# A fourth projection unit loaded ahead into its own place, and a new order on VectorE and ScalarE around decay and sparse scores

## The chip, the cores and the metric

The kernel runs on one core of a Trainium2 chip. The metric is the device time of one execution in microseconds (us), the median of three runs. The engines of the core work side by side, each with its own queue of instructions: TensorE (PE: matmuls; PEld: the loads of their stationary operand), VectorE (DVE), ScalarE (ACT), GpSimd (POOL) and SyncE (SP). SP and POOL issue the transfers (DMAs) from device memory that this case is about. Engines wait for each other through semaphores.

## What is computed

Two layers over 256 tokens of width 1024, all in fp32. The change lies in the first, whose shape is:

```python
mod = jax.nn.silu(c) @ mod_w + mod_b                  # shift, scale, gate, twice
h = rms_norm(x, g_pre_mix) * (1 + scale1) + shift1
(sc_b, sc_c, sc_x, q, k, v, z, xbc, dt_raw, gl_a, gl_b, gl_c) = split_columns(h @ w_in)
y_a = short_conv_mixer(sc_b, sc_c, sc_x, sc_conv_w) @ w_sc_out
y_b = stick_breaking_attention(q, k, v) @ w_sb_out     # log-sigmoid scores, cumulated, exp
y_c = mamba2_mixer(z, xbc, dt_raw, ...) @ w_ssm_out    # conv, silu, decay matrix, scores, y * silu(z), norm
merged = sigmoid(gl_a) * y_a + sigmoid(gl_b) * y_b + sigmoid(gl_c) * y_c
x = x + gate1 * rms_norm(merged @ w_o, g_post_mix)
h2 = rms_norm(x, g_pre_ffn) * (1 + scale2) + shift2
x = x + gate2 * rms_norm((silu(gt) * up) @ w_ffn_out, g_post_ffn)
```

The second layer has attention, pooling, and a mixture of single experts: for each token and each of 8 heads 16 rows of an expert table are fetched, multiplied with the token and added up.

## The kernel before

**Units of weights.** All weights of the projections come as units of 128 x 2048 fp32 values (1 MiB), in the order of the list ORDER: xbc 0 to 2, sc 0 to 2, qk 0 and 1, v, z 0 and 1, gl 0 to 11, then br 0 to 3 (output projections of the three branches), wo 0 to 3, and the feed-forward units gu and dn. Unit u lies in slot u % 3 of `ring`. SP loads a unit when the unit three before it is done (`load`, L422: it waits for `unit_done`, which TensorE raises once per unit). FRONT0 is the unit sc 0. The first three loads (`first_load`) wait for nothing.

**Three passes.** The xbc units are multiplied as plain fp32 (L619). From sc 0 to gl 11 each unit is split: ScalarE writes a rounded high half (`split_front`, L1216, in two halves), VectorE the remainder (`front_lo`, L1824, over the unit in the ring), and TensorE makes three products low x high, high x low, high x high (`proj_T`, lines L509 to L511, 48 matmuls of 256 columns each with their weight loads). ScalarE copies each result out of its accumulator bank (`copy_out`, L1199) and raises `evac`; TensorE may run two units ahead of that copy.

**Modulation.** `mod_w` is 48 further units of 1 MiB. VectorE multiplies each with silu(c) and sums (`mod_unit`: two `mod_dot`, L1747). Units 0 to 7 come among SP's first loads (`load_pair(0)` to `load_pair(3)`) and give the scale and shift of h: two columns of hT for each pair (`early_columns`), which ScalarE then makes from x (`hT_part`, L1187). From unit 8 on POOL loads them (`load_mods`, L1551) into the two buffers of `mod_ring`: unit m is issued when unit m-2 has been summed. Units 8 to 19 are needed by `modulation(8, 20)`, 20 to 27 later.

**The start.** `transposes(0)` brings x into eight chunks k; chunks 2j and 2j+1 of hT follow pair j. `xbc_part(j, *ks)` makes the matmuls of xbc j over the chunks ks. `products_in_pause(n, ...)` makes n plain fp32 products whose result nobody uses, so that TensorE has work where it would wait. Then ScalarE rounds all of hT (`hq_h`, L1250) and VectorE makes the rest (`hq_l`, L1828). After sc 0 come the 32 small matmuls for dt (L642).

**Order on VectorE and ScalarE.** It is written out by hand. VectorE goes through the convolution of xbc, dt, the short convolution, the sparse scores (`sbl`, `sba`), the decay (L1944 to L1958), y and its norm (`yc`, `ysq`), then the merging of the branches (L2030 to L2039) in the loop over br; between these stand the `front_lo` of the coming units and the `mod_unit`s. In the decay, VectorE makes 16 arguments from a matmul (`acs_mm`, L719/L720, signalled by `dec_arg`), ScalarE takes exp (L1315), TensorE makes the scores of B and C (`bc_mm`, after gl 7, when all 16 arguments are read), VectorE multiplies (L1958, `w_ready`), and TensorE makes y from it after gl 8 (L738, `y_mm`). The sum of squares (L748) follows gl 9. TensorE's br j needs the low half of its own unit (`split_br`) and from j = 2 on the merged result of br j-2; wo 0 needs merged 0 to 2 and its low half (`split_wo`, L2016).

ScalarE takes for the sparse scores Abs, Exp, then the split of gl 0, then Ln (`sb_log`), and only then copies z 0 out, with Silu.

Of the kernel before, what the change touches and what calls it, by code (L numbers as in the profile page):

```python
# [127 lines left out]
def build(nc, stream, mod_w, c_rows, small, x, band, final_g, experts, out):  # L128
    with ExitStack() as ctx:
# [144 lines left out]
        w_lo = [rounded(f"w_lo{s}", "areaB", s * UNIT, UNIT) for s in range(RING)]  # L274
        front_hi = [rounded(f"front_hi{n}", *at, UNIT)
                    for n, at in enumerate((("spare", 0), ("xn", 0), ("gate_area", 4096), ("areaB", 6144)))]
        ring_lo = [rounded(f"ring_lo{s}", "ring", s * UNIT, UNIT) for s in range(RING)]
        yc_h, yc_l = rounded("yc_h", "areaA", 2048, 4, T), rounded("yc_l", "areaA", 3072, 4, T)
# [120 lines left out]
        def _(sp):  # L399
# [12 lines left out]
            sp.dma_start(sm[:, 0:n_late], small[:, 0:n_late]).then_inc(small_in, 16)  # L412
            load_pair(1)
            first_load(0)
            load_pair(2)
            first_load(1)
            load_pair(3)
            first_load(2)
# [16 lines left out]
            for i in range(1, edge):  # L435
                for s in range(RING):
                    load(i, s, False)
# [36 lines left out]
        def _(pe):  # L474
            mm = nc.tensor.matmul

            def arrived(kind, j):
                u = AT[kind, j]
                if kind == "wq":
                    pe.wait_ge(*query_arrived(j))  # L480
                    return query_w[j]
                if (kind, j) == ("wo2", 2):
                    pe.wait_ge(wo2_in, 16)
                    return spare[:, :]
                pe.wait_ge(w_in[u % RING], 16 * (u // RING + 1))
                return slot[u % RING]
# [47 lines left out]
            def front_parts(u, half):  # L534

                if u == FRONT0:
                    pe.wait_ge(hq_lo_ready, 1)
                pe.wait_ge(front_lo_ready, 2 * (u - FRONT0) + half + 1)
                return front_high(u), ring_lo[u % RING]
# [85 lines left out]
            products_in_pause(5, 1, xn[:, 0, 0:T])  # L625
            xbc_part(0, 2, 3)
            xbc_part(1, 0, 1)
            products_in_pause(4, BX, xn[:, 0, 0:T])
            xbc_part(1, 2, 3)
            xbc_part(0, 4, 5)  # L630
            xbc_part(1, 4, 5)
            xbc_part(2, 0, 1)
            xbc_part(2, 2, 3)
            xbc_part(0, 6, 7)
            xbc_part(1, 6, 7)
            xbc_part(2, 4, 5, 6, 7)
# [497 lines left out]
        def _(act):  # L1134
# [66 lines left out]
            def split_hi(u, i=0):  # L1201

                act.wait_ge(w_in[u % RING], i * 16 + 16 * (u // RING + 1))
                if u >= SPLIT0 + RING:
                    act.wait_ge(unit_done, i * RING + (u - RING + 1))
                A(w_hi[u % RING], slot[u % RING], ACT.Identity).then_inc(hi_ready, 1)  # L1206

            def split_front(u):

                act.wait_ge(w_in[u % RING], 16 * (u // RING + 1))  # L1210
                if u > FRONT0:
                    act.wait_ge(unit_done, u - RING + 1)
                if u == AT["gl", 9]:
                    act.wait_ge(acs_mm, 2)
                for half in halves_of_unit:
                    A(front_high(u)[:, half], slot[u % RING][:, half], ACT.Identity).then_inc(front_hi_ready, 1)  # L1216

            def split_br(j):

                u = AT["br", j]  # L1220
                act.wait_ge(w_in[u % RING], 16 * (u // RING + 1))
                A(br_hi[j], slot[u % RING][:, UNIT // 2:], ACT.Identity).then_inc(front_hi_ready, 1)

            def split_wo(j):

                u = AT["wo", j]
                act.wait_ge(w_in[u % RING], 16 * (u // RING + 1))
                for half in (slice(0, UNIT // 2), slice(UNIT // 2, UNIT)):
                    A(wo_hi[j][:, half], slot[u % RING][:, half], ACT.Identity).then_inc(front_hi_ready, 1)
# [21 lines left out]
            n = 0  # L1251
            for j in range(3):
                if j == 2:
                    split_front(FRONT0)
# [27 lines left out]
            step.wait()  # L1282
            A(sbl, sbl, ACT.Ln, bias=1.0).then_inc(sb_log, 1)
            for j in range(2):
                copy_out("z", j, zg[:, 2 * j:2 * j + 2, :], func=ACT.Silu, bank=n % 2)
                if j == 0:
                    split_front(n + 3)
                n += 1
            for b in range(6):
# [259 lines left out]
        def _(pool):  # L1549
# [8 lines left out]

            load_mods(MOD_SP, MOD_FRONT + 2)
# [92 lines left out]
        def _(dve):  # L1652
# [166 lines left out]
            def front_lo(kind, j):  # L1819

                u = AT[kind, j]
                for h, half in enumerate(halves_of_unit):
                    dve.wait_ge(front_hi_ready, 2 * (u - FRONT0) + h + 1)
                    V.tensor_tensor(ring_lo[u % RING][:, half], slot[u % RING][:, half],  # L1824
# [4 lines left out]

            for k in range(4):  # L1830
# [5 lines left out]
                for b in range(6):  # L1836
                    w = c_("ssm_w", 4 * b + k, 4 * b + k + 1)
                    if (k, b) == (0, 4):
                        front_lo("sc", 0)
# [121 lines left out]
            mod_unit(21)  # L1961
            front_lo("gl", 10)
            mod_unit(22)
# [10 lines left out]
            mod_unit(23)  # L1974
# [30 lines left out]
            mod_units(24, 26)  # L2005
# [568 lines left out]
```

## Time and profile before

| | us |
|---|---|
| median of 3 runs | 1218.07 |
| the runs | 1217.13, 1218.07, 1776.78 |
| the profiled execution, its own time | 1217.03 |
| its span, first to last instruction | 1215.4 |
| granted clock of TensorE, mean of full speed | 0.972 |
| TensorE busy (matmul) | 1072.5 |
| VectorE busy | 875.8 |
| ScalarE busy | 517.5 |

One of the three runs was disturbed. The page gives busy times and the chain that ended last; the trace behind it can be asked for windows, waits and single instructions. In what follows a time like 160.2 us counts from the start of the span of the profiled execution. The durations of matmuls are modelled: their starts are the sounder figure.

### The profile page before, as it was taken

The numbers are of one execution on the slowest core, as the hardware profiler recorded it, in microseconds if no ns is written. First come the engines' busy times: TensorE is split into PE (matmuls) and PEld (weight loads), VectorE is DVE, ScalarE is ACT, GpSimd is POOL, SyncE is SP. The second block draws the span as 40 slices with busy tenths as digits, with TensorE's granted clock in tenths as the row PEclk, the third lists the DMA queues.
The fourth block names the chain that finished last, engine by engine and source line by source line (L and its number), as shares of the span: only waits on it lengthen the run. The fifth ranks groups of instructions, "written<-read, shape, count | busy, mean of one in ns | idle before, by whom it ended". The sixth has DMA issues, their size and how long they took to land.

```text
span 1215.4 us, 14124 instructions
## 1 busy us (share of the span) xinstructions
PE 1072.5 (88%) x4834; PEld 715.7 (59%) x4834; DVE 875.8 (72%) x1802; ACT 517.5 (43%) x1156; POOL 339.2 (28%) x326
## 2 busy tenths in 40 slices
PE   3899979999999999998999999977968878769776
PEld 3899969878999989765565555422323323223222
DVE  5668789977888887737797758668577586685455
ACT  3338443364333345435544344433434334334344
POOL 0000100031000002203544545634434535334320
PEclk9899999999999999999999999999999998999998
DMA  9756966565888882557999999999999999999994
GB/s 380 301 194 228 366 252 242 210 250 204 313 308 321 316 318 108 212 208 289 421 410 421 423 419 421 421 421 422 421 421 422 421 421 423 420 422 421 420 422 197
DMA packets 57946, 414.10 MB, mean 341 GB/s; under 512 B 6432, under 2 KB 6432, under 8 KB 8352
## 3 DMA queue, kind: packets, MB, share of 16 engines
q0 software_dynamic: 43632, 313.02, 63.0%
q1 hardware_dynamic: 14112, 100.10, 21.9%
q8 instruction: 30, 0.49, 0.2%
q10 hardware_dynamic: 144, 0.26, 0.1%
q14 instruction: 28, 0.23, 0.1%
HBM read 412.30 MB, written 1.05 MB: 340 GB/s over the span
## 4 chain that ended last, share of the span: by engine, by line
PE 53%; DMA 31%; DVE 9%; ACT 5%; issue 1%; POOL 0%; SPq 0%; ACTq 0%; DVEq 0%; POOLq 0%
PE ps L1064 15%; PE ps L509 8%; PE ps L510 8%; PE ps L511 8%; DMA areas_seam<-in_experts,idx 6%; DMA gate_area<-in_experts,idx 6%; DMA spare<-in_experts,idx 6%; PE ps L495 4%; DMA ring<-in_stream 3%; DMA mod_ring<-in_experts,idx 3%; DMA ring<-in_experts,idx 3%; DMA ring<-in_experts,part_buf 2%; PE ps L765 1%; PE ps L991 1%; PE ps L619 1%
## 5 line engine op out<-in xcount | busy, mean ns | idle before, releaser
L1485 ACT ACTIVATE act<-now 128x1 f32<-128x1 f32 x256 | 50.7, 198 | 264.3 <-DVE now L2369 262.0
L1064 PE MATMUL ps<-areaB,c_row 128*128 128x512 f32 x232 | 116.1, 633 | 26.1 <-ACT c_row L1493 26.1
L1493 ACT ACTIVATE c_row<-small,act 128x128 f32<-128x128 f32 x256 | 102.8, 402 | 16.3 <-ACT act L1489 0.8
L1747 DVE CUSTOM_DVE_ANT_0 mod_ring<-mod_ring,c_row 128x1024 f32<-128x1024 f32 x84 | 99.1, 1219 | 14.6 <-DMA mod_ring<-in_mod_w 14.5
L1064 PE MATMUL ps<-ring,c_row 128*128 128x512 f32 x192 | 92.8, 614 | 14.4 <-ACT c_row L1493 13.8
L1623 POOL DMA_INDIRECT areaB<-in_experts,idx x58 | 65.3, 1126 | 124.5 <-PE ps L1064 65.8
L509 PE MATMUL ps<-hT_h,w_lo 128*128 128x256 f32 x352 | 99.1, 282 | 0.8 <-DVE hid_l L2062 0.8
L511 PE MATMUL ps<-hT_h,w_hi 128*128 128x256 f32 x352 | 98.9, 281 | 0.0
L510 PE MATMUL ps<-hT_l,w_hi 128*128 128x256 f32 x352 | 98.8, 281 | 0.0
L2369 DVE CUSTOM_DVE_ANT_0 areaB<-areaB,xn 128x1024 f32<-128x1024 f32 x58 | 70.7, 1224 | 37.3 <-DMA areaB<-in_experts,idx 37.2
L1064 PEld LDWEIGHTS ps<-areaB,c_row 128*128 128x128 f32 x232 | 43.6, 197 | 90.9 <-ACT c_row L1493 47.1
L1206 ACT ACTIVATE w_hi<-ring 128x2048 fp32r<-128x2048 f32 x41 | 78.4, 1913 | 40.7 <-PE ps L511 38.0
L509 PE MATMUL ps<-hq_h,ring_lo 128*128 128x256 f32 x304 | 88.9, 293 | 4.6 <-DVE ring_lo L1824 3.5
L1064 PE MATMUL ps<-gate_area,c_row 128*128 128x512 f32 x156 | 75.4, 606 | 13.9 <-ACT c_row L1493 13.9
L510 PE MATMUL ps<-hq_l,front_hi 128*128 128x256 f32 x304 | 87.3, 287 | 0.0
L511 PE MATMUL ps<-hq_h,front_hi 128*128 128x256 f32 x304 | 87.0, 286 | 0.0
L2369 DVE CUSTOM_DVE_ANT_0 ring<-ring,xn 128x1024 f32<-128x1024 f32 x48 | 58.4, 1225 | 31.2 <-DMA ring<-in_experts,idx 31.1
L1760 DVE TENSOR_TENSOR w_lo<-ring,w_hi 128x2048 fp32r<-128x2048 f32 x30 | 68.7, 2292 | 16.3 <-ACT w_hi L1206 16.3
L1489 ACT ACTIVATE act<-act,gate_buf 128x1 f32<-128x1 f32 x256 | 75.4, 295 | 9.3
L1555 POOL DMA_DIRECT2D mod_ring<-in_mod_w x22 | 11.8, 538 | 235.1 <-DVE modT L1747 235.1
L1064 PEld LDWEIGHTS ps<-ring,c_row 128*128 128x128 f32 x192 | 35.5, 194 | 66.2 <-issue 35.8
L1623 POOL DMA_INDIRECT ring<-in_experts,idx x47 | 54.9, 1168 | 65.9 <-PE ps L1064 52.2
(436 smaller groups left out, 2591.7 us busy)
## 6 DMA issues: line engine op xcount, KB each, us to landing
ring<-in_stream SPq DMA_DIRECT2D x75, 1024.0 KB, 5.0
mod_ring<-in_mod_w POOLq DMA_DIRECT2D x40, 1024.0 KB, 5.3
gate_area<-in_mod_w SPq DMA_DIRECT2D x3, 1024.0 KB, 14.7
areaB<-in_mod_w SPq DMA_DIRECT2D x3, 1024.0 KB, 24.6
gate_area<-in_stream SPq DMA_DIRECT2D x3, 1024.0 KB, 13.0
mod_ring<-in_mod_w SPq DMA_DIRECT2D x2, 1024.0 KB, 7.6
small<-in_small SPq DMA_DIRECT2D x1, 1352.0 KB, 28.6
c_row<-in_c_rows SPq DMA_DIRECT2D x2, 512.0 KB, 17.4
```

The source lines that it names most:

```text
L509: mm(o, lhs[1], rhs[0], start=start, stop=False, **kw)
L510: mm(o, lhs[0], rhs[1], start=False, stop=False, **kw)
L511: return mm(o, lhs[0], rhs[0], start=False, stop=stop, **kw)
L1064: last = mm(ps[:, B3 + 2 * b + t, :], spread_w[n // FEW % 2][:, n % FEW, :], row[ROW_OF[n]][:, D + 512 * b:D + 512 * b + 512], start=first ...
L1206: A(w_hi[u % RING], slot[u % RING], ACT.Identity).then_inc(hi_ready, 1)
L1485: A(weight, now[n // FEW % 4][:, here], ACT.Gelu).then_inc(gelu_done, 1)
L1489: step(A(weight, weight, ACT.Identity, scale=gate_h[h % 2][:, t, n % TOPK:n % TOPK + 1]))
L1493: A(spread_w[n // FEW % 2][:, n % FEW, :], c_("ident"), ACT.Identity, scale=weight)\
L1623: pool.indirect_dma_start(row[ROW_OF[n]], None, experts, bass.IndirectOffsetOnAxis(ap=idx[:, n:n + 1], axis=0))\
L1747: V.tensor_tensor_reduce(w, w, silu, 1.0, 0.0, ALU.mult, ALU.add, column).then_inc(mod_summed, 1)
L1760: V.tensor_tensor(w_lo[s], slot[s], w_hi[s].bitcast(F32), ALU.subtract).then_inc(lo_dve, 1)
L2369: V.tensor_tensor_reduce(u, u, xn[:, t, :], 1.0, 0.0, ALU.mult, ALU.add, now[n // FEW % 4][:, n % FEW:n % FEW + 1]).then_inc(dot_done, 1)
```

## The change

- sc 0 gets a place of its own, `fourth` in areaB at 6144 (the place of `a_rep`, which is written only later), and its load stands among the first loads, behind the last pair of modulation units; it signals `wo2_in`. `w_arrived(u)` gives the semaphore and count for each unit. The next load of slot 0 is that of qk 0, still issued when sc 0 is done.
- SP's first loads: xbc 0 now before pair 1, xbc 1 and 2 before pair 2.
- TensorE's xbc parts are ordered by chunks: all three units get chunks 0 to 3, then 4 and 5, then 6 and 7; the pause products are 3, 3 and 3 instead of 5 and 4.
- ScalarE splits sc 0 before it copies xbc out; z 0 is copied (without Silu) before the Ln of the sparse scores, z 1 after the split of gl 1, and one Silu goes over both.
- POOL waits for `unit_done` 3 (all xbc units) before it loads modulation unit 8.
- VectorE makes the low half of gl 8 before the decay arguments. Units 19 and 20 no longer stand between arguments and products. The new places: 19 after the low half of gl 9, 20 to 22 between `split_br(0)` and `split_br(1)`, 23, 24, 25 in the branch loop. 26 and 27 stay.

```diff
+        fourth = cut(areaB, 6144, UNIT)
+        fourth_lo = rounded("fourth_lo", "areaB", 6144, UNIT)
...
+        def w_arrived(u):
+
+            if u == FRONT0:
+                return wo2_in, 16
+            return w_in[u % RING], 16 * (u // RING + 1) - (16 if u > FRONT0 and u % RING == FRONT0 % RING else 0)
...
             sp.dma_start(sm[:, 0:n_late], small[:, 0:n_late]).then_inc(small_in, 16)
+            first_load(0)
             load_pair(1)
-            first_load(0)
+            first_load(1)
+            first_load(2)
             load_pair(2)
-            first_load(1)
             load_pair(3)
-            first_load(2)
+            sp.dma_start(fourth, stream[FRONT0]).then_inc(wo2_in, 16)
...
-            for i in range(1, edge):
-                for s in range(RING):
-                    load(i, s, False)
+            for n in range(FRONT0 + 1, RING * edge):
+                load(n // RING, n % RING, False)
...
             xbc_part(0, 0, 1)
-            products_in_pause(5, 1, xn[:, 0, 0:T])
             xbc_part(0, 2, 3)
+            products_in_pause(3, 1, xn[:, 0, 0:T])
             xbc_part(1, 0, 1)
-            products_in_pause(4, BX, xn[:, 0, 0:T])
             xbc_part(1, 2, 3)
-            xbc_part(0, 4, 5)
-            xbc_part(1, 4, 5)
+            products_in_pause(3, BX, xn[:, 0, 0:T])
             xbc_part(2, 0, 1)
             xbc_part(2, 2, 3)
-            xbc_part(0, 6, 7)
-            xbc_part(1, 6, 7)
-            xbc_part(2, 4, 5, 6, 7)
+            products_in_pause(3, 2, xn[:, 0, 0:T])
+            for j in range(3):
+                xbc_part(j, 4, 5)
+            for j in range(3):
+                xbc_part(j, 6, 7)
...
+            split_front(FRONT0)
             for j in range(3):
-                if j == 2:
-                    split_front(FRONT0)
                 copy_out("xbc", j, xbc_raw[:, 2 * j:2 * j + 2, 3:], bank=(0, 1, BX)[j])
...
             split_front(AT["gl", 0])
-            step.wait()
-            A(sbl, sbl, ACT.Ln, bias=1.0).then_inc(sb_log, 1)
             for j in range(2):
-                copy_out("z", j, zg[:, 2 * j:2 * j + 2, :], func=ACT.Silu, bank=n % 2)
+                if j == 1:
+                    split_front(n + 2)
+                copy_out("z", j, zg[:, 2 * j:2 * j + 2, :], bank=n % 2)
                 if j == 0:
-                    split_front(n + 3)
+                    act.wait_ge(act_step, step.n)
+                    A(sbl, sbl, ACT.Ln, bias=1.0).then_inc(sb_log, 1)
                 n += 1
+            act.wait_ge(evac, n)
+            step(A(zg, zg, ACT.Silu))
...
+            pool.wait_ge(unit_done, 3)
             load_mods(MOD_SP, MOD_FRONT + 2)
...
+            front_lo("sc", 0)
             for k in range(4):
...
+            front_lo("gl", 7)
             mod_unit(18)
-            front_lo("gl", 7)
+            front_lo("gl", 8)
...
-            front_lo("gl", 8)
-            mod_units(19, 21)
             dve.wait_ge(bc_mm, 1)
             for h in range(8):
-                if h == 4:
-                    front_lo("gl", 9)
...
-            mod_unit(21)
+            front_lo("gl", 9)
+            mod_unit(19)
             front_lo("gl", 10)
-            mod_unit(22)
             dve.wait_ge(y_mm, 1)
...
             front_lo("gl", 11)
-            mod_unit(23)
...
             split_br(0)
-            mod_units(24, 26)
+            mod_units(20, 23)
             split_br(1)
...
             for j in range(4):
                 if j in (1, 2):
                     split_br(j + 1)
+                if j == 1:
+                    mod_unit(23)
+                if j == 2:
+                    mod_unit(24)
                 if j == 3:
+                    mod_unit(25)
                     split_wo(0)
```

## Rows read from the trace of the kernel before

**Rows 1.** Page: the chain that ended last, by engine, share of the span.

```profile
PE 53%; DMA 31%; DVE 9%; ACT 5%; issue 1%; POOL 0%; SPq 0%; ACTq 0%; DVEq 0%; POOLq 0%
```

**Rows 2.** Windows: length, busy us (xcount) by engine, granted clock, DMA share, GB/s.

```profile
760.00:1215.00 455.00, 356.89 (x730) 135.97 (x728) 298.18 (x709) 179.74 (x562) 183.87 (x171) 0.95 0.98 407
```

**Rows 3.** Two waits of TensorE, 100 to 180 us: total us, times, longest.

```profile
PE ps L509 <- ACT areaA L1199: 1.0, 1, 1.0
...
PE ps L738 <- DVE areaB L1958: 7.2, 1, 7.2
```

**Rows 4.** Windows of the front stages, same columns.

```profile
160.00:201.60 41.60, 33.98 (x270) 31.91 (x269) 40.60 (x73) 17.15 (x17) 2.64 (x5) 0.92 0.62 224
201.60:246.20 44.60, 43.97 (x246) 37.79 (x245) 43.48 (x63) 14.77 (x16) 1.58 (x3) 1.00 0.61 227
60.00:160.00 100.00, 98.85 (x801) 96.20 (x799) 72.05 (x109) 55.54 (x66) 5.82 (x11) 0.98 0.71 270
```

**Rows 5.** Timeline of the start: start us, us, engine, line, operation [idle before].

```profile
23.95 1.02 ACT L1187 ACTIVATE hT<-ps,cols 128x256 f32<-128x256 f32 x2 [2.65 <-DVE cols L1786]
...
26.50 1.23 DVE L1747 CUSTOM_DVE_ANT_0 areaB<-areaB,c_row 128x1024 f32<-128x1024 f32 x1
...
31.47 1.23 DVE L1747 CUSTOM_DVE_ANT_0 areaB<-areaB,c_row 128x1024 f32<-128x1024 f32 x1 [2.05 <-DMA areaB<-in_mod_w]
...
32.56 15.70 PE L619 MATMUL ps<-hT,ring 128*128 128x256 f32 x72
...
36.97 1.02 ACT L1187 ACTIVATE hT<-ps,cols 128x256 f32<-128x256 f32 x2 [6.44 <-DVE cols L1786]
...
39.97 2.29 DVE L1828 TENSOR_TENSOR hq_l<-hT,hq_h 128x2048 fp32r<-128x2048 f32 x1 [3.09 <-ACT hq_h L1250]
...
51.79 0.55 PE L509 MATMUL ps<-hq_h,ring_lo 128*128 128x256 f32 x1 [3.52 <-DVE ring_lo L1824]
```

**Rows 6.** Windows around two waits, then two matmuls of the chain.

```profile
54.00:57.00 3.00, 3.00 (x16) 3.00 (x15) 3.00 (x7) 1.15 (x2) 0.00 (x0) 0.50 0.06 25
...
179.80:182.00 2.20, 2.13 (x12) 1.55 (x14) 2.20 (x4) 0.01 (x1) 0.00 (x0) 0.50 0.60 242
...
52.34 0.21 PE ps L510
...
57.57 0.12 PE ps L511
```

**Rows 7.** ScalarE's copy of z 0, from its timeline.

```profile
107.53 0.60 ACT L1199 ACTIVATE areaA<-ps 128x512 f32<-128x512 f32 x1
```

**Rows 8.** A wait of VectorE, 60 to 246 us: total us, times, longest.

```profile
DVE mod_ring L1747 <- DMA mod_ring<-in_mod_w: 7.5, 4, 3.0
```

**Rows 9.** The mod_ring loads: landing times, one issue on POOL, its first product.

```profile
DMA to landing us min/median/max: 5.0/6.5/9.1
...
120.41 0.53 POOL L1555 DMA_DIRECT2D mod_ring<-in_mod_w  x1 [11.99 <-DVE modT L1747]
...
127.26 1.23 DVE L1747 CUSTOM_DVE_ANT_0 mod_ring<-mod_ring,c_row 128x1024 f32<-128x1024 f32 x1 [3.01 <-DMA mod_ring<-in_mod_w]
```

**Rows 10.** VectorE's timeline, then two pieces of the chain.

```profile
139.07 2.35 DVE L1824 TENSOR_TENSOR ring_lo<-ring,front_hi 128x1024 fp32r<-128x1024 f32 x2
...
160.20 0.48 DVE L1944 SCALAR_TENSOR_TENSOR areaB<-ps,dtb,small 128x256 f32<-128x256 f32 x1 [3.48 <-PE ps L720]
...
227.92 2.35 DVE L2016 TENSOR_TENSOR ring_lo<-ring,wo_hi 128x1024 fp32r<-128x1024 f32 x2
...
167.76 1.13 DVE mod_ring L1747
...
172.34 2.60 DVE areaB L1958 x8
```

**Rows 11.** Chain of work before gl 5, and behind wo 1.

```profile
140.76 0.44 PE ps L691 x4
...
241.90 4.88 DMA ring<-in_stream
```

More of the change, by code:

```diff
@@ L277, in build, with front_slot, front_low @@
         ring_lo = [rounded(f"ring_lo{s}", "ring", s * UNIT, UNIT) for s in range(RING)]
+        fourth_lo = rounded("fourth_lo", "areaB", 6144, UNIT)
+        def front_slot(u):
+            return fourth if u == FRONT0 else slot[u % RING]
+        def front_low(u):
+            return fourth_lo if u == FRONT0 else ring_lo[u % RING]
+        def w_arrived(u):
+            if u == FRONT0:
+                return wo2_in, 16
+            return w_in[u % RING], 16 * (u // RING + 1) - (16 if u > FRONT0 and u % RING == FRONT0 % RING else 0)
         yc_h, yc_l = rounded("yc_h", "areaA", 2048, 4, T), rounded("yc_l", "areaA", 3072, 4, T)
@@ L482, in arrived @@
                 if (kind, j) == ("wo2", 2):
-                    pe.wait_ge(wo2_in, 16)
+                    pe.wait_ge(wo2_in, 32)
                     return spare[:, :]
-                pe.wait_ge(w_in[u % RING], 16 * (u // RING + 1))
+                pe.wait_ge(*w_arrived(u))
                 return slot[u % RING]
@@ L538, in front_parts @@
                 pe.wait_ge(front_lo_ready, 2 * (u - FRONT0) + half + 1)
-                return front_high(u), ring_lo[u % RING]
+                return front_high(u), front_low(u)
             def proj_T(kind, j):
@@ L1201, in split_hi @@
             def split_hi(u, i=0):
-                act.wait_ge(w_in[u % RING], i * 16 + 16 * (u // RING + 1))
+                act.wait_ge(w_in[u % RING], i * 16 + w_arrived(u)[1])
                 if u >= SPLIT0 + RING:
@@ L1208, in split_front @@
             def split_front(u):
-                act.wait_ge(w_in[u % RING], 16 * (u // RING + 1))
+                act.wait_ge(*w_arrived(u))
                 if u > FRONT0:
@@ L1215, in split_front @@
                 for half in halves_of_unit:
-                    A(front_high(u)[:, half], slot[u % RING][:, half], ACT.Identity).then_inc(front_hi_ready, 1)
+                    A(front_high(u)[:, half], front_slot(u)[:, half], ACT.Identity).then_inc(front_hi_ready, 1)
             def split_br(j):
                 u = AT["br", j]
-                act.wait_ge(w_in[u % RING], 16 * (u // RING + 1))
+                act.wait_ge(*w_arrived(u))
                 A(br_hi[j], slot[u % RING][:, UNIT // 2:], ACT.Identity).then_inc(front_hi_ready, 1)
@@ L1226, in split_wo @@
                 u = AT["wo", j]
-                act.wait_ge(w_in[u % RING], 16 * (u // RING + 1))
+                act.wait_ge(*w_arrived(u))
                 for half in (slice(0, UNIT // 2), slice(UNIT // 2, UNIT)):
@@ L1823, in front_lo @@
                     dve.wait_ge(front_hi_ready, 2 * (u - FRONT0) + h + 1)
-                    V.tensor_tensor(ring_lo[u % RING][:, half], slot[u % RING][:, half],
+                    V.tensor_tensor(front_low(u)[:, half], front_slot(u)[:, half],
                                     front_high(u)[:, half].bitcast(F32), ALU.subtract).then_inc(front_lo_ready, 1)
@@ L1837, in _ @@
                     w = c_("ssm_w", 4 * b + k, 4 * b + k + 1)
-                    if (k, b) == (0, 4):
-                        front_lo("sc", 0)
                     if k == 0:
```

## The prediction

> **What bounds the kernel now.** I began with the page: the chain that ended last [rows 1]. TensorE carries just over half of the chain, the DMAs under a third, VectorE 9%. An average like that hides stages, so I cut the span next. In the window of the gather stage, from 760 us to the end, the DMA share is 0.98 at 407 GB/s [rows 2]: there the transfers of expert rows set the time, their bytes are fixed, and only when they start can move. Everything the change touches lies before 250 us, so its worth is how much earlier (or later) that part ends; the feed-forward stage and the gathers then pass the shift on unchanged. That is my assumption for all that follows.
>
> In the first 250 us, who waits for whom is short to tell. TensorE waits three times: 3.5 us for the low half of sc 0, 1.0 us for ScalarE's copy of z 0, 7.2 us for VectorE's decay products [rows 3, 5]. Windows by stage show the other side of it: from 60 to 160 us TensorE is busy 98.9 of 100 us and VectorE only 72, but from 160.0 to 201.6 VectorE is busy 40.6 of 41.6 and from 201.6 to 246.2 it is busy 43.5 of 44.6, while TensorE is busy 44.0 of that [rows 4]. So the first stage is TensorE's, and the stage from the decay to the output projection is VectorE's, with TensorE only just kept fed. Time that TensorE wins before 160 us can be kept; time that it wins after 160 us is kept only if VectorE ends earlier too.
>
> **Part 1: sc 0 in a place of its own.** Before, its load can be issued only when xbc 0 has freed the slot; ScalarE and VectorE split it only after that, and TensorE, done with xbc at 48.26, starts on it at 51.79, 3.52 us late [rows 5]. What would the new order of loads do? The 1 MiB loads go through in the order of issue at about 420 GB/s, 2.5 us each: modulation units 5 and 6 stand two loads apart in the queue and their first products start at 26.50 and 31.47, 5.0 us apart [rows 5]. The three xbc units and two pairs now stand ahead of the last pair, so the last modulation unit lands one load (2.5 us) later than before, and the last columns of hT come 2.5 us later: before they start at 36.97, after at about 39.5, ready by 40.6. Does TensorE wait for them? Its xbc work is the same 96 passes plus the same 9 pause products (5+4 before, 3+3+3 after) of 2 passes each at 0.217 us (15.70 us for 72 [rows 5]). The second pair of columns started at 23.95 before [rows 5]; its unit too lands one load later, but VectorE had come late to it, so the first of them is there at about 25.1. From then 106 passes remain, 23.0 us: the end is 48.1, the same as before, and the passes that need the last columns begin at 42.9, 2.3 us after these are there. hT's copy (1.9 us, to 42.5), its low half (2.3 us, to 44.9) and the first low half of sc 0 (to 46.1) also fit under it. So sc 0 starts at 48.1: 3.7 us gained.
>
> The pause costs more than itself. After it the granted clock stood at 0.50, the 1.2 GHz level, until about 57.2 us; matmuls of sc 0 follow each other at 0.21 us and then at 0.12 [rows 6]. Some 25 of its 48 ran at the slow pace: 25 x 0.09 = 2.3 us; with the long first one 2.5. Without the pause I take the clock to stay up. Part 1 is worth 3.7 + 2.5 = 6.2 us at 60 us. Behind it sc 1 and sc 2 (issued as before, at about 46 and 48) share the DMAs with the modulation units 8 and 9, which now wait for unit_done 3 on POOL's queue: 4.2 MB at 420 GB/s from 48 us are in by 58, and sc 2 is wanted at 63. Nothing is late.
>
> **Part 2: z and sparse scores on ScalarE.** The copy of z 0 now precedes the logarithm and its table load; before it ended at 108.1 behind them [rows 7] and TensorE waited 1.0 us [rows 3]. After: no wait. But the logarithm ends some 0.5 us later, the separate Silu over zg is one ACTIVATE of about 1.1 us more, and on VectorE modulation units 11 and 12 then end 1.0 us later, so the loads of 13 and 15 (each issued when its buffer is free) land 1 us later. VectorE was already waiting on such loads four times, 7.5 us [rows 8]. The low half of gl 5 stands behind unit 15 and was started 1.7 us ahead of TensorE (139.07 [rows 10], against the transposes ahead of gl 5 at 140.76 [rows 11]); with the sum and the load each 1 us later it is now about 0.9 late. I take the 1.0 us as given back: 0, with a bound of -1.0.
>
> **Part 3: the decay on VectorE.** The low half of gl 8 (2 halves, 2.3 us) moves from behind the decay arguments into the 3.5 us that VectorE waits for TensorE before 160.2 [rows 10]: cover enough. Units 19 and 20 (4 dots, 4.6 us [rows 10]) and the low half of gl 9 leave the way to the decay products, so these are there 5.2 us (2 x 2.60 [rows 10]) after the scores of B and C, before gl 8 ends on TensorE. The 7.2 us wait goes; so does the slow clock behind it (0.50 at 180 us [rows 6]), 1.5 us (16 + 16 passes of small products at twice their time, 4.6 us in place of about 3.1); and 0.4 us ahead of the sums of squares. By TensorE alone this is worth 9 us.
>
> VectorE's account says otherwise. From the first decay argument (160.20) to the first low half of wo 0 (229.1 [rows 10]) it has 68.9 us. The change takes 2.3 us out (gl 8), and adds nothing: units 19 to 25 stood in this stretch before and stand in it after, only later (20, 21, 22 between the two first branch splits, 23, 24, 25 in the branch loop). It adds two waits. First 1.3 us for the matmuls of B and C, because VectorE now comes there with nothing between. Then the three units in a row: mod_ring has two buffers, the load of unit 22 is issued only when unit 20 is summed, some 0.8 us after it, and lands 6.4 us later (the row: issued at 120.41, first product at 127.26, 6.85 us; median of all 6.5 [rows 9]). Unit 21 covers 2.3 us of it, so VectorE stands 0.8 + 6.4 - 2.3 = 4.9 us. Bounds: 0.8 + 5.0 - 2.3 = 3.5, and 0.8 + 9.1 - 2.3 = 7.6 from the shortest and longest landing. Sum: 68.9 - 2.3 + 1.3 + 4.9 = 72.8 us, 3.9 more than before; with the 0.35 us that TensorE was behind VectorE here, 3.5. The Trainium skill gives a fit for such a load in "DMA: Bandwidth & Descriptors", Anatomy of one DMA: about 2.0 us plus bytes over 436e3. It comes to 4.4 us for 1 MiB, no load of this row group was that fast, and by it the sum would be 2.0 us smaller.
>
> TensorE meanwhile finishes gl 11 some 8 us earlier, and stands in the branch stage: 2.4 us for the low half of br 1, 2.5 and 1.7 us for the merges, and about 5 us for the first half of wo 0. Only the last reaches the end. The pauses of 3.5 and of 7.2 us both had the clock at 0.50 behind them [rows 6], so I expect wo 0 to begin at 1.2 GHz. Price: between 1.5 us (the decay pause) and 2.5 (the first pause), I take 2.1. Behind it the chain is as before: wo 1 frees the slot, gu 0 loads in 4.9 us [rows 11].
>
> **Sum.** -6.2 (part 1) + 0 (part 2) + 3.5 (VectorE) + 2.1 (clock) = -0.6 us. Against the profiled run of 1217.03 us (span 1215.4) that is 1216.4; the two undisturbed timed runs lie 0.1 and 1.0 above the profiled one, so I forecast 1217.0 for the median. The likeliest case's own range is 1214 to 1219.
>
> **The rivals.**
> - *The early start is kept.* Unit 22 lands in time for unit 21's end, or the clock stays up in wo 0, or both: -0.6 - 4.9 - 2.1 = -7.6, so 1209.4 to 1215. For it: the DMA share was only 0.6 in these windows [rows 4]. Against: VectorE did wait for such loads with one unit in hand.
> - *TensorE is the bound and all its waits count.* 6.2 + 1.0 + 7.2 + 1.5 + 0.4 = 16.3: 1200.7. Against it: VectorE has 2 us of idle time in the 86 us of [rows 4].
> - *Slower: unit 22 comes late.* If it lands 9.1 us after issue as the longest [rows 9], VectorE stands 7.6 us and the sum is -0.6 + 2.7 = +2.1, with the clock's price at its upper bound 0.4 more: 1217.0 + 2.7 + 0.4 = 1220.1. It decides from a landing of 7.0 us on; POOL's loads then share with br 2 and br 3 of SP's queue, which speaks for it.
> - *Part 1 does nothing.* The last columns of hT are more than 2.3 us later than reckoned, or sc 1 then stalls instead: -0.6 + 6.2, 1222.6.
>
> **How the numbers follow.** Likeliest 0.50; early start kept 0.23; TensorE the bound 0.08; unit 22 late 0.13; part 1 without effect 0.06. The range 1209 to 1221 leaves out the second rival and the last, 0.14, and the tails. Two per cent, about what a measurement of this kernel can tell from no change, is 24 us, more than any case moves: faster 0.03, same 0.95, slower 0.02 stand for what I have not thought of.
>
> **What would show it.** Part 1: TensorE without a wait at 48 us, clock 1.00 from 46 to 54, sc 0's copy out near 54. Part 3: no wait before the decay products; in its place a wait of VectorE for a mod_ring load of 4 to 5 us shortly after the first branch split, and TensorE waits before br 2, br 3 and wo 0, the last with the clock at 0.5 behind it. The forecast is wrong if VectorE's stretch from the first decay argument to the first low half of wo 0 is under 70 us, or if sc 0 does not start by 49 us.

## The result and the profile after

| us | before | after |
|---|---|---|
| median | 1216.47 (20 runs, 1213.09 to 1776.78) | 1218.99 (20 runs, 1215.32 to 1222.07) |
| the profiled execution, its own time | 1217.03 | 1217.65 |
| its span | 1215.4 | 1215.8 |
| granted clock, mean | 0.972 | 0.973 |

One run of before (1776.78) and one of a_spread below (2730.70) were disturbed, and the ratios leave them out. The ratio after to before is 1.0021, 95% interval 1.0012 to 1.0029: the change costs 2.5 us. The forecast was 1217.0 within 1209 to 1221, a change of -0.6 us; the range holds, the sign doesn't. The gain of the first part is there, and the two losses that the forecast set against it are there too. When the load of gu 0 is issued, after is still ahead of before. What the forecast lacked is that this load, taken as unchanged, now takes 3.6 us longer.

The two profiled executions lie closer together (0.6 us) than the medians. They serve to see where time goes; what the change costs is read from the ratio.

The page's chain that ended last, by engine, has moved from TensorE to VectorE (compare [rows 1]: PE 53, DVE 9):

```profile
PE 50%; DMA 31%; DVE 12%; ACT 4%; issue 2%; POOL 0%; SPq 0%; ACTq 0%; POOLq 0%; DVEq 0%
```

Windows of after: length, busy us (xcount) of PE, PEld, DVE, ACT, POOL, granted clock, DMA share, GB/s. They answer to [rows 4] and to the first of [rows 6].

```profile
60.00:160.00 100.00, 99.70 (x812) 96.78 (x811) 78.09 (x123) 62.30 (x72) 5.83 (x11) 0.99 0.71 266
160.00:201.60 41.60, 38.41 (x296) 36.23 (x295) 35.75 (x59) 15.49 (x17) 2.12 (x4) 1.00 0.60 225
201.60:246.20 44.60, 34.48 (x171) 28.40 (x170) 40.81 (x59) 10.18 (x11) 2.65 (x5) 0.96 0.65 238
46.00:54.00 8.00, 8.00 (x62) 7.74 (x60) 6.23 (x14) 3.21 (x4) 1.26 (x2) 1.00 0.79 308
54.00:57.00 3.00, 3.00 (x29) 3.00 (x28) 2.28 (x3) 2.13 (x3) 0.00 (x0) 1.00 1.03 437
```

From 46 to 57 us TensorE has no gap, and its granted clock is 1.00 where it was 0.50. In the third row TensorE has 34.5 us of work in 44.6, 9.5 us less than before in that window: it stands there now. The waits of TensorE, 40 to 262 us, say for whom (total us, times, longest):

```profile
PE ps L525 <- DVE ring_lo L2030: 5.0, 1, 5.0
PE ps L781 <- DVE hT_l L2058: 4.1, 2, 2.6
PE ps L810 <- DVE xn L1725: 3.9, 2, 3.3
PE ps L764 <- DVE areaB L1987: 1.8, 1, 1.8
PE ps L525 <- DVE ring_lo L2015: 1.4, 1, 1.4
```

The 7.2 and 3.5 us of [rows 3, 5] are gone. In their place stand 5.0 us for the low half of wo 0, 4.1 for the merges, 1.8 ahead of the sums of squares (0.4 before), 1.4 for br 1, and 3.3 us of the third row behind wo, where it was 0.17 before. The last is TensorE waiting for what follows gu 0's high half. Single instructions of after, VectorE first, then GpSimd, then ScalarE (start us, us, engine, line, operation [idle before]):

```profile
153.15 0.49 DVE L1963 SCALAR_TENSOR_TENSOR areaB<-ps,dtb,small 128x256 f32<-128x256 f32 x1 [3.48 <-PE ps L736]
...
196.97 1.23 DVE L1766 CUSTOM_DVE_ANT_0 mod_ring<-mod_ring,c_row 128x1024 f32<-128x1024 f32 x1 [4.34 <-DMA mod_ring<-in_mod_w]
...
224.41 2.35 DVE L2030 TENSOR_TENSOR ring_lo<-ring,wo_hi 128x1024 fp32r<-128x1024 f32 x2
...
238.92 0.53 POOL L1573 DMA_DIRECT2D mod_ring<-in_mod_w  x1 [13.16 <-DVE modT L1766]
...
247.87 1.92 ACT L1222 ACTIVATE w_hi<-ring 128x2048 fp32r<-128x2048 f32 x1 [5.76 <-DMA ring<-in_stream]
```

And four pieces of the chain that ended last (start us, us, what): the start of wo 0, one of its later matmuls, and the load of gu 0.

```profile
225.78 0.77 PE ps L525
226.55 0.43 PE ps L526
...
229.17 0.23 PE ps L527
...
239.33 8.46 DMA ring<-in_stream
```

At the issue of gu 0's load after is 2.6 us ahead of before (239.33 against 241.90 [rows 11]). The load then takes 8.46 us in place of 4.88, and when ScalarE makes the high half of gu 0 (247.87; before 246.86) the kernel is 1.0 us behind. The same instructions before:

```profile
242.42 0.53 POOL L1555 DMA_DIRECT2D mod_ring<-in_mod_w  x1 [31.43 <-DVE modT L1747]
...
246.86 1.92 ACT L1206 ACTIVATE w_hi<-ring 128x2048 fp32r<-128x2048 f32 x1 [2.64 <-DMA ring<-in_stream]
```

Before, GpSimd's load of modulation unit 28 was issued at 242.42, 0.5 us behind that of gu 0. After, it is issued at 238.92, 0.4 us ahead of it. Measured from the low half of wo 0, GpSimd's issue hasn't moved (14.5 us behind it in both, since VectorE sums unit 26 in the same place); SyncE's has, from 13.98 to 14.92 us, since TensorE goes through wo 0 and wo 1 more slowly (below).

### The profile page after: what moved, and what is told of

Same layout as the page of the kernel before. It is cut to its first block, busy times and chain, and to the rows that moved or that the text cites. A ratio compares the mean times of both kernels' runs of the same rounds, so it can differ in the third digit from the quotient of the medians.

```text
span 1215.8 us, 14136 instructions
## 1 busy us (share of the span) xinstructions
PE 1072.7 (88%) x4834; PEld 714.9 (59%) x4834; DVE 876.1 (72%) x1802; ACT 518.7 (43%) x1157; POOL 340.4 (28%) x326
## 3 DMA queue, kind: packets, MB, share of 16 engines
HBM read 412.30 MB, written 1.05 MB: 340 GB/s over the span
## 4 chain that ended last, share of the span: by engine, by line
PE 50%; DMA 31%; DVE 12%; ACT 4%; issue 2%; POOL 0%; SPq 0%; ACTq 0%; POOLq 0%; DVEq 0%
PE ps L1080 15%; PE ps L525 8%; PE ps L526 7%; PE ps L527 7%; DMA areas_seam<-in_experts,idx 6%; DMA gate_area<-in_experts,idx 6%; DMA spare<-in_experts,idx 6%; PE ps L511 4%; DMA mod_ring<-in_experts,idx 3%; DMA ring<-in_experts,idx 3%; DMA ring<-in_experts,part_buf 2%; DMA ring<-in_stream 2%; PE ps L635 2%; DMA gate_area<-in_mod_w 1%; DVE mod_ring L1766 1%
## 5 line engine op out<-in xcount | busy, mean ns | idle before, releaser
L1080 PE MATMUL ps<-ring,c_row 128*128 128x512 f32 x192 | 95.7, 630 | 14.3 <-ACT c_row L1511 13.7
L525 PE MATMUL ps<-hq_h,ring_lo 128*128 128x256 f32 x288 | 83.1, 289 | 0.1
```

The lines of the kernel that those rows point to most:

```text
L525: mm(o, lhs[1], rhs[0], start=start, stop=False, **kw)
L1080: last = mm(ps[:, B3 + 2 * b + t, :], spread_w[n // FEW % 2][:, n % FEW, :], row[ROW_OF[n]][:, D + 512 * b:D + 512 * b + 512], start=first ...
```

## The experiments

Three theories stood behind the runs. **A**, the forecast's account: part 1 pays, and VectorE's late load of unit 22 and the slow clock of wo 0 take it back. **B**: the loads of unit 28 and of gu 0 collide, 3 to 4 us that A doesn't have. **C**, for later runs: the stage from the decay to wo 0 is bound by VectorE's work, or by its idle time, or by TensorE. Every ratio is against runs of before on the same chip; the instants are those of one profiled execution each. The difference of two ratios has an interval of its own. From the intervals of the table I estimate 1.7 to 2.0 us either way for the kernels made from after against after, and 2.7 to 3.1 us for those made from p1 among each other.

| kernel | median us | ratio to before, 95% | first decay argument | low half of wo 0 | high half of gu 0 |
|---|---|---|---|---|---|
| before | 1216.5 | 1 | 160.20 | 227.92 | 246.86 |
| after | 1218.99 | 1.0021 (1.0012, 1.0029) | 153.15 | 224.41 | 247.87 |
| p1 | 1211.35 | 0.9952 (0.9932, 0.9971) | 154.14 | 221.89 | 240.78 |
| p12 | 1211.75 | 0.9954 (0.9938, 0.9971) | 154.00 | 221.73 | 240.55 |
| p3 | 1227.14 | 1.0076 (1.0057, 1.0094) | 160.74 | 234.80 | 258.54 |
| a_spread | 1214.37 | 0.9978 (0.9967, 0.9990) | 154.04 | 220.88 | 244.26 |
| a_hold | 1221.86 | 1.0040 (1.0027, 1.0052) | 154.30 | 225.87 | 246.09 |
| a_issue | 1216.92 | 1.0003 (0.9990, 1.0016) | 152.79 | 224.76 | 244.42 |
| a_both | 1210.96 | 0.9958 (0.9944, 0.9972) | 153.46 | 220.27 | 240.37 |
| p1_g8 | 1207.79 | 0.9924 (0.9907, 0.9941) | 154.12 | 219.59 | 238.39 |
| g8_coll | 1210.92 | 0.9951 (0.9937, 0.9966) | 154.62 | 220.08 | 241.25 |
| g8_m19 | 1208.87 | 0.9936 (0.9920, 0.9951) | 159.04 | 222.19 | 240.91 |
| v_less | 1209.35 | 0.9948 (0.9933, 0.9963) | 153.44 | 220.81 | 239.74 |

### Part 1 alone, part 3 alone, parts 1 and 2

**p1**: the kernel before with the place of sc 0, the order of loads and of xbc, and GpSimd's wait; VectorE's order of decay and units, and ScalarE's of z, as before.

> Part 1 alone on the kernel before: sc 0 in its own place, the new order of the first loads and of the xbc parts, POOL's wait; VectorE's and ScalarE's later order as before. Theory A (VectorE's order after 160 us, with its wait for unit 22, gives the gain of part 1 back): this kernel keeps the 6 us, about 1210.5 against 1216.5, and wo 1 ends near 235.7 instead of 241.9. Theory C (the early start itself is worth nothing at the end, or later stages absorb it): no difference from before within 1 us.

5.8 us faster than before (0.9952), with all of the three instants of the table some 6.0 us earlier: 6.06, 6.03, 6.08. What part 1 gains before 60 us is carried through whole.

**p3**: only VectorE's new order on the kernel before.

> VectorE's order alone on the kernel before (gl 8 ahead of the decay arguments, units 19 to 25 later). Theory A: no wait for the decay products, but the stretch from the first decay argument to the first low half of wo 0 grows from 68.9 to about 72.8 us and wo 0 starts with the clock at half: 4 to 6 us slower than before. Theory B (the loss is made at the end of wo, where gu 0's load now shares the DMAs with unit 28's): 3 to 4 us more on top, gu 0 landing 8 us after its issue, so 8 to 9 us slower. Theory C (the order is worth its 7 us of TensorE): faster by up to 7 us.

1.0076, 9.2 us slower. VectorE waits 5.6 us for unit 22, and the low half of wo 0 is 6.9 us later than before; from there to gu 0's high half it is 23.7 us in place of 18.9, 4.8 us more. So VectorE's new order loses in two places, before wo 0 and behind it: A and B together, and part 3 is what makes the whole change slow. Part 1 and part 3 add up to -5.8 + 9.2 = +3.4, near the +2.5 of the whole.

**p12**: p1 with ScalarE's order of z and the sparse scores.

```diff
-            step.wait()
-            A(sbl, sbl, ACT.Ln, bias=1.0).then_inc(sb_log, 1)
             for j in range(2):
+                if j == 1:
+                    split_front(n + 2)
-                copy_out("z", j, zg[:, 2 * j:2 * j + 2, :], func=ACT.Silu, bank=n % 2)
+                copy_out("z", j, zg[:, 2 * j:2 * j + 2, :], bank=n % 2)
                 if j == 0:
+                    act.wait_ge(act_step, step.n)
+                    A(sbl, sbl, ACT.Ln, bias=1.0).then_inc(sb_log, 1)
-                    split_front(n + 3)
                 n += 1
+            act.wait_ge(evac, n)
+            step(A(zg, zg, ACT.Silu))
```

> The first part and the second together (the copy of z 0 ahead of the logarithm, one Silu over zg), VectorE's order as before; the first part alone ran at 1211.35 us. Theory A (the prediction's step: the 1.0 us is given back on the way to gl 5): 1211.4, and the first decay argument starts at 154.0 to 154.3 as with the first part alone (154.14). Theory B (it is kept, since the changed kernel's first decay argument stood 7.05 us earlier than before, where the first part gives 6.1): 153.2 to 153.4, and 1210.5 us. Told apart too by TensorE's wait for ScalarE near 113 us: none under B.

0.9954 against 0.9952: part 2 is worth nothing that these runs can tell, as forecast. The reason is another than the forecast's. The wait of 1.0 us for z 0's copy, which part 2 was to win, isn't there in p1 any more. In its place TensorE waits 0.8 us at 113 us for ScalarE's copy of gl 0, and in p12 it is 0.7 us (in after, with the same order on ScalarE, there is none). At gl 5, where the forecast had the gain given back, p12 shows no wait. The 7.05 us at the first decay argument of after was one execution: in the kernels with part 1 but without part 2 this instant lies between 153.44 and 154.62 (g8_m19 apart, for a reason told below), in those with both between 152.79 and 154.30.

### Is the wait for unit 22 what VectorE's order costs?

**a_spread**: after, with unit 20 put ahead of the sums of squares, and 21 and 22 left between the branch splits.

```diff
             front_lo("gl", 11)
+            mod_unit(20)
             dve.wait_ge(ysum_mm, 1)
...
-            mod_units(20, 23)
+            mod_units(21, 23)
```

> The changed kernel with unit 20 moved ahead of the wait for the sum of squares, so that only 21 and 22 stand between the first two branch splits and unit 22's load is issued earlier. Theory A: VectorE's 4.3 us wait for unit 22 goes, wo 0 starts 4 us earlier, the wait ahead of it is under 1.5 us and the clock stays up: 5 to 7 us faster than the changed kernel, about 1212.5. Theory B (only the collision of gu 0 and unit 28 counts): wo 1 ends earlier, but unit 28 is issued earlier by as much, the 8.5 us landing stays: at most 4 us faster.

0.9978, 5.2 us faster than after by the ratios. VectorE has no wait for unit 22 any more, and from the first decay argument to the low half of wo 0 it needs 66.8 us, after 71.3: the 4.3 us of that wait are the 4.4 us saved. TensorE's wait before wo 0 stays 5.0 us, against what I expected. It has nothing to do with unit 22. In after the merge of br 1 ends at 214.2, when TensorE starts br 3; VectorE then has a split of br 3 (1.14), unit 24 (2.3), merge 2 (4.6), unit 25 (2.3) and half a split (1.15), 11.4 us, and TensorE some 6.5 us for br 3. So I put this wait down to the units placed in the branch loop: the two units are 4.6 of VectorE's 11.4 us. That is read from the trace; no run moved these units alone.

### The collision of two loads

**a_hold**: after, with GpSimd issuing the loads of units 28 and 29 together, only behind its own part of gu 0.

```diff
-            load_mods(MOD_SP, MOD_FRONT + 2)
+            load_mods(MOD_SP, MOD_FRONT)
...
             split_lo(SPLIT0)
+            load_mods(MOD_FRONT, MOD_FRONT + 2)
```

> The changed kernel with the loads of units 28 and 29 held on POOL until ScalarE has made gu 0's high half, so that gu 0 has the DMAs to itself. Theory A: wo 1's end is what counts, the load is 5 us as before or little more: under 1 us of difference from the changed kernel. Theory B: gu 0 lands in 5 us instead of 8.5, everything behind it comes 3.5 us earlier: about 1215.5 against 1219.

1.0040, slower than after by 2.3 us. gu 0 itself is cured: its load takes 4.8 us, and the high half comes 20.2 us behind the low half of wo 0 (after 23.5). But the two held loads are then issued at 250.9 and meet the load of gu 1, issued at 251.83 and landed 9.3 us later. The high half of gu 1 waits until 261.17 (with after's distance of 12.9 us to that of gu 0 it would be 259.0), and TensorE waits 2.4 us at 263.7. The collision was moved by one unit, not removed; this run didn't separate the theories.

**a_issue**: the same idea, cleaner.

```diff
-            load_mods(MOD_SP, MOD_FRONT + 2)
+            load_mods(MOD_SP, MOD_FRONT)
+            pool.wait_ge(*w_arrived(SPLIT0))
+            load_mods(MOD_FRONT, MOD_FRONT + 2)
```

> The changed kernel, and GpSimd issues the load of modulation unit 28 only when gu 0 is in; units 28 and 29 then follow one by one as their buffers come free. Theory B (the collision of unit 28's load with gu 0's costs 3 us): gu 0 lands 4.9 us after its issue, its high half starts near 244.8 instead of 247.9, 1215.9 us. Theory A (what was lost there is not the order of the two loads but the total traffic): gu 0 still takes over 7 us, 1219.

1.0003: 2.2 us better than after by the ratios. The load of gu 0 takes 4.66 us (expected 4.9), the two held loads are issued together at 245.01 and not one by one, and from the low half of wo 0 to gu 0's high half it is 19.7 us in place of 23.5. B is confirmed in place by the trace, and 2.2 us agrees with its 3 us within the interval:

```profile
239.68 4.66 DMA ring<-in_stream
```

**a_both**: a_spread and a_issue together.

> The changed kernel with unit 20 ahead of the sums of squares, units 21 and 22 around the second branch split, and unit 28's load only when gu 0 is in. If the two losses are separate they add up: 4.6 (first, alone 1214.4) and 2.2 to 3.1 (second, alone 1216.9), 1211.3 to 1212.2 us, and what is left above the first part with gl 8 moved (1207.8) is the wait of 5.0 us before wo 0 with its slow clock. If they are one and the same loss: 1214.4.

0.9958: 7.7 us better than after, where the two alone gave 5.2 and 2.2. The losses are separate and add up within the intervals, and this kernel, with after's order of the decay and the branch loop, is as fast as p1. To p1_g8 below, 2.0 us remain at gu 0's high half, and another 1.5 us come behind it, in a stretch told at the end.

**g8_coll** turns it around: in a kernel without the collision (p1_g8, below) SyncE waits until unit 28's load has been issued. So that it can, GpSimd raises `pool_go` behind each load in place of ahead of it; nothing else waits for `pool_go`.

```diff
+                if n == SPLIT0:
+                    sp.wait_ge(pool_go, MOD_FRONT + 1 - MOD_SP)
...
-                        pool.sem_inc(pool_go, 1)
                         pool.dma_start(cut(mod_ring, n * UNIT, UNIT),
                                        mod_w[bass.ds(2 * i + n, 1)].rearrange("o p n -> p (o n)"))\
                             .then_inc(mod_in[n], 16)
+                        pool.sem_inc(pool_go, 1)
```

> The first part with the low half of gl 8 moved (1207.8 us), and SyncE issues the load of gu 0 only after GpSimd has issued that of modulation unit 28; without this wait gu 0 was issued at 233.56 and unit 28 at 234.10, so the order of the two turns around and gu 0 is issued some 0.6 us later. Nothing else is changed. Theory B (whichever of the two is issued second lands late, and the feed-forward stage starts with gu 0): gu 0 takes about 8.5 us in place of 4.75, so 0.6 + 3.7 = 4.3 us more, 1212.1. Theory A (what was lost in the changed kernel is not due to the order of the two loads): 0.6 us more, 1208.4.

0.9951 against 0.9924, 3.3 us (expected 4.3). GpSimd issued at 234.50, SyncE at 234.52. The chain has gu 0's load with 6.65 us there, against 4.75 in p1_g8:

```profile
234.52 6.65 DMA ring<-in_stream
```

```profile
233.56 4.75 DMA ring<-in_stream
```

Turning the order around by 0.6 us costs 1.9 us of landing, and the wait for GpSimd makes the issue itself some 0.5 us later. All kernels together, by how long unit 28's load was issued ahead of gu 0's:

| unit 28 ahead of gu 0 by | kernels | gu 0 lands after, us | unit 28 lands after, us |
|---|---|---|---|
| -0.5 us (behind it) | before, p1, p12, p1_g8, g8_m19, v_less | 4.68 to 4.88 | 7.9 to 8.0 |
| 0.02 | g8_coll | 6.65 | 8.5 |
| 0.4 | after | 8.46 | 7.9 |
| 0.8 | a_spread | 7.97 | 5.0 |
| 1.7 | p3 | 7.46 | 5.0 |
| held back until gu 0 is in | a_hold, a_issue, a_both | 4.66 to 4.85 | issued in a pair with unit 29 |

So the price jumps at equal issue and falls slowly as the other load gets a longer lead. A load that is 0.8 us or more ahead lands in 5.0 us and the other pays; close to equal issue both are late. The four rows from 0.02 to 1.7 are one execution each, so the shape between these points is not shown.

In all kernels in which nothing holds GpSimd back, unit 28's issue stands 14.4 or 14.5 us behind the low half of wo 0, VectorE's instant. It is gu 0's, TensorE's instant, that varies: 14.0 us behind it in the six kernels of the first row, where wo 0 starts without a wait, and 14.9 in after, 15.3 in a_spread, 16.2 in p3, where wo 0 starts after 5.0 us of standing, at half clock.

### What bounds the stage from the decay to wo 0

**p1_g8**: p1, and of part 3 only the low half of gl 8 ahead of the decay arguments, in VectorE's idle time.

```diff
+            front_lo("gl", 8)
             dve.wait_ge(acs_mm, 2)
             dve.wait_ge(acs_read, 1)
...
-            front_lo("gl", 8)
             mod_units(19, 21)
```

> The first part, and of the third one piece alone: the low half of gl 8 (2.3 us of VectorE) is made before the decay arguments, where VectorE stood idle for 3.5 us, instead of behind them. All modulation units stay where they stood. Theory A (VectorE's busy time plus its idle time sets the end of this stage; what went wrong in the whole change is the idle time that came in with the late load of unit 22): 2.3 us less than the first part alone, 1209.1 us, first low half of wo 0 at 219.6 (221.89 with the first part alone). Theory B (only waits of TensorE count, and the wait before the decay products just becomes shorter by what TensorE then loses elsewhere): 1211.3, low half of wo 0 at 221.9.

0.9924: 3.4 us faster than p1 by the ratios, 9.2 us faster than before, the lowest ratio of all. The low half of wo 0 is 2.30 us earlier than in p1, exactly the length of what was moved. TensorE's wait before the decay products falls from 7.2 to 5.0 us: both engines gain the same piece. The other 1.5 us of the profiled execution come later and are told below.

**v_less**: p1, but four dots of units 22 and 23 over half their columns, 2.4 us of VectorE's work left out, with part of the modulation not computed.

```diff
+                n = D // 2 if m in (22, 23) else D
-                w = mod_place(m)[:, D * b:D * b + D]
-                silu = c_row[:, D * (m // 24):D * (m // 24) + D]
+                w = mod_place(m)[:, D * b:D * b + n]
+                silu = c_row[:, D * (m // 24):D * (m // 24) + n]
```

> The first part, with the four dots of modulation units 22 and 23 over 512 of their 1024 columns only (the other half of these products is left out); their loads are the same. That takes 4 x 0.6 = 2.4 us of work from VectorE between the decay and wo 0 and none from any other engine. Theory A (VectorE sets the end of that stage): 2.4 us less than the first part alone, 1209.0. Theory B (TensorE or the loads set it): 1211.3.

0.9948 against 0.9952: no difference to be seen, but with 3 us either way the timed runs don't exclude 2.4 us. The profiled executions, one each, say more. From the first decay argument to the low half of wo 0 it is 67.4 us, in p1 67.75: of 2.4 us only 0.4 arrive. In their place VectorE waits three times 0.5 us for TensorE's products of br 0 to 2:

```profile
DVE areaB L2046 <- PE ps L527: 1.5, 3, 0.5
```

So neither of this run's theories is right alone: VectorE and TensorE reach wo 0 within half a microsecond of each other, and work taken from VectorE *behind* the decay products, where TensorE doesn't wait, brings only 0.4 us. In p1_g8 the piece stood *ahead* of the products, on both engines' way.

**g8_m19**: p1_g8 with unit 19 too ahead of the decay arguments.

```diff
             front_lo("gl", 8)
+            mod_unit(19)
             dve.wait_ge(acs_mm, 2)
...
-            mod_units(19, 21)
+            mod_unit(20)
```

> The first part with the low half of gl 8 moved (1207.8 us), and modulation unit 19 (2.3 us) too ahead of the decay arguments, where VectorE still stood idle for 2.47 us; its load was issued at 143.82 and is there. Theory A (this idle time is still worth its length): 2.3 us less, 1205.5; TensorE's wait before the decay products falls from 5.0 to 2.7. Theory C (with half the units' work taken out behind the decay TensorE had only some 0.4 us less to do until wo 0, so TensorE sets the end there; but here its own wait becomes shorter): also 2.3 less. Rival: the idle time is already worth nothing, 1207.8.

0.9936, not faster than p1_g8; 2.3 us less would be 0.9905, below the interval of this run, though p1_g8's own interval makes that a weak exclusion. The profiled execution shows the first decay argument 4.9 us late, behind a wait for the load of unit 18 that stands *ahead* of everything this edit moves:

```profile
149.91 1.23 DVE L1763 CUSTOM_DVE_ANT_0 mod_ring<-mod_ring,c_row 128x1024 f32<-128x1024 f32 x1 [6.09 <-DMA mod_ring<-in_mod_w]
```

That load was issued at 139.91 and took 9.97 us on the chain, beside a load of SyncE's issued 1.05 us behind it. In p1_g8 it was issued at 139.27, 1.55 us ahead of SyncE's, and landed in 5.4 us; its first product starts at 144.72. So a lead of about 1 us doesn't always save the load that is ahead. The fuller order has no slack left to take up such a load, as the 2.5 us of idle time had. Whether the other executions lost their time in the same way is open, and so is whether the idle time was worth its length: this run didn't put the question to the test.

## Why the prediction was right and wrong

**Part 1: right.** The last columns of hT start at 39.51 (forecast 39.5), sc 0 at 47.93 (forecast 48.1), and the clock stays at 1.00 until 57. The first matmul of sc 1 starts at 57.43 in place of 63.66, 6.2 us earlier, and p1 gains 5.8 to 6.1 us against 6.2. The rival that part 1 does nothing is out. Behind the matmuls for dt both kernels have a stretch with the granted clock at 0.50 (from 64 to 67.6 us before, from 58 to 61.5 after), so it takes nothing from the gain. One sign failed without a cost: sc 0's copy starts at 56.78, not near 54, since ScalarE splits sc 1 and sc 2 first.

**Part 2: right in size, not in its reason.** Worth 0, but the wait that it was to win isn't there any more beside part 1, and the late start of gl 5 that was to take the gain back doesn't show in p12.

**VectorE's account: right.** Forecast 72.8 us from the first decay argument to the first low half of wo 0; the trace has 153.15 to 225.65, 72.5. Its two added waits are 1.27 (forecast 1.3) and 4.34 us (forecast 4.9), the latter with a landing of 5.9 us (191.08 to 196.94; by [rows 9] between the shortest, 5.0, and the median, 6.5). By the estimate of 4.4 us that the fit in the Trainium skill's "DMA: Bandwidth & Descriptors", Anatomy of one DMA, gives for 1 MiB the wait would have been 2.9 us; the measurement decides, and no load of [rows 9] came that early.

**TensorE's waits: right in place, the first 1.0 us too long.** They are 1.4, 2.6, 1.5 and 5.0 us, forecast 2.4, 2.5, 1.7 and about 5. The wait ahead of the sums of squares, 0.4 us before, was to go and grew to 1.8 us instead. That VectorE's account alone gave the end was partly luck. In after TensorE does wait for VectorE at wo 0, but in p1 and v_less the two engines are level within half a microsecond, and by VectorE's account alone the 2.4 us taken out in v_less would have been priced at 2.4 us, where 0.4 came.

**The clock at wo 0: mechanism right, size off.** The forecast took a price between 1.5 and 2.5 us and chose 2.1. Matmuls of 512 columns run at 0.43 us until 228.68 and at 0.23 behind it; five at 0.20 more and a first one of 0.77 in place of 0.31 before make 1.5 us. That is the lower bound. Of the 3.66 us by which wo 0 starts earlier 2.57 are left at gu 0's issue, so 1.1 us net reached the end.

**The failed step** is the last sentence of the sum's working: behind wo 0 "the chain is as before: wo 1 frees the slot, gu 0 loads in 4.9 us". It took 8.46 us, 3.6 more than the term allowed, and no rival had it either. I had set the slow clock of wo 0 into the sum as 2.1 us and then let the chain go on "as before", but a chain that is later against VectorE is not as before: GpSimd's issues follow VectorE, SyncE's follow TensorE, and the two issues stood only 0.5 us apart. TensorE's 0.9 to 1.1 us of slow clock turned their order around. So VectorE's longer stretch before wo 0 was paid three times: in its own 3.5 us, in the clock, and in the load, which cost as much again as the first. a_issue (the collision removed), g8_coll (put into a kernel without it) and a_both (it adds up with the other loss) show the late load as a cause of its own; that the clock sets the order is read from the distances above, no run kept the clock up with everything else as it was. With 3.6 us added, and the clock at 1.1 in place of 2.1, the sum is -0.6 + 3.6 - 1.0 = +2.0, against the +2.5 measured by the ratio.

The two profiled executions alone give less, 1.0 us at gu 0's high half: after is 7.05 us ahead at the first decay argument, loses 3.4 up to the start of wo 0, 1.1 up to gu 0's issue and 3.6 in the load. The distance to +2.0 is that its first decay argument was early, by 7.05 us where the sum has 6.2. The +2.0 itself lies within the measured interval, 1.5 to 3.5 us.

**Sums and base.** The forecast's time rests on a base of 1217.6 us without the change, from two timed runs; over 20 runs before has 1216.47. From that same base three rivals' times should be 1210.0, 1201.3 and 1223.2, where the prediction has 1209.4, 1200.7 and 1222.6. Nothing in the outcome hangs on these 0.6 us.

The rival that ended on the slow side, unit 22 late, has the sign but not the cause: unit 22 landed 5.9 us after its issue, not 9.1.

## What to carry to other kernels

When an edit moves work that frees a buffer, list the loads that this buffer's release will issue, on every queue, do the same for an engine that the edit makes later or slower, and set the new instants against the issue of the transfer that the chain waits for. A load of the same size issued 0.5 us behind gu 0's cost it nothing here; issued level or ahead it cost 2 to 4 us. Fill an engine's idle time ahead of a meeting point, where both engines gain; where two engines are level, taking work from one behind that point gave 0.4 us of 2.4. And take the parts of a compound change alone: part 1 with one small piece of part 3 was 9.2 us faster than before, where the whole was 2.5 us slower.

## What was new of the hardware

The same sequence of matmuls with the same waits can lose the clock in one kernel and keep it in another. At the start of the second norm's projection p1 and p1_g8 have identical waits of TensorE, 0.57, 0.31, 0.95 and 0.82 us, 2.39 us apart in time. In p1 a stretch behind them runs at half clock, in p1_g8 none does (windows, p1 first, then p1_g8):

```profile
260.00:263.00 3.00, 3.00 (x16) 3.00 (x16) 2.79 (x7) 2.38 (x2) 3.00 (x4) 0.51 0.75 306
```

```profile
257.00:260.00 3.00, 2.91 (x24) 2.91 (x25) 2.79 (x7) 2.98 (x2) 3.00 (x5) 1.00 0.84 309
```

That is the other 1.5 us between these two profiled executions. The stretch from gu 0's high half to the third high half after it is 30.3 us in p1 and 28.8 in p1_g8. The other kernels fall into the same two groups: 30.1 to 30.3 us in before, after, p12, a_issue and a_both, and 28.7 to 29.0 in g8_coll, g8_m19, v_less, p3 and a_spread; a_hold, with its moved collision, has 33.2. So small gains can be followed by a step of 1.5 us either way, for which no row here gives a reason, and of what p1_g8 gains over p1 in the profiled executions 1.5 us are this step.
